# A transformer kernel's SwiGLU input stages: a seed copied ahead of a SiLU, and the first stage's norm, low parts and gates reordered

## What is computed

```python
def swiglu(x, w_in, w_out):
    a, b = jnp.split(x @ w_in, 2, axis=-1)
    return (jax.nn.silu(a) * b) @ w_out

for i in range(DEPTH_2):
    h = h + FFN_RES * swiglu(rmsnorm(h, g_ff1[i]), w_ff1_in[i], w_ff1_out[i])
    h = h + hybrid_mixer(rmsnorm(h, g_mix[i]), ...)
    h = h + FFN_RES * swiglu(rmsnorm(h, g_ff2[i]), w_ff2_in[i], w_ff2_out[i])
    ...
```

## Time and profile before

| | us |
|---|---|
| median of 3 runs | 2997.67 |
| lowest and highest | 2995.54, 3002.64 |
| the profiled execution, device time | 2998.98 |
| its span in the trace | 2997.0 |
| TensorE busy | 2900.9 (97%) |
| VectorE busy | 2123.1 (71%) |
| ScalarE busy | 1396.3 (47%) |
| mean granted TensorE clock | 0.988 |

### The profile page before, as it was taken

The page is one execution under the profiler, slowest core; times in us unless marked ns, Lnnn a source line. Parts: engine busy times, 40 slices in busy tenths (PEclk is TensorE's granted clock), DMA queues, the critical chain, the costliest instruction groups (busy, mean ns, idle before and its releaser), DMA issues. The chain is left out here.

```text
span 2997.0 us, 50791 instructions
## 1 busy us (share of the span) xinstructions
PE 2900.9 (97%) x18548; PEld 2500.2 (83%) x18548; DVE 2123.1 (71%) x3185; ACT 1396.3 (47%) x2309; POOL 455.9 (15%) x356
## 2 busy tenths in 40 slices
PE   7999999889999999999999999999999999999998
PEld 3888888777789988777799988799888777899886
DVE  5677776355689745887699845899547886899545
ACT  3645555454356522334466522566323335566422
POOL 0113112184600011000300012100110000200012
PEclk9999999999999999999999999999999999999998
DMA  6212022123223222322232323233222222323322
GB/s 258 62 44 63 24 55 59 36 81 117 99 88 112 97 98 81 98 92 77 98 107 98 115 88 112 71 112 99 100 89 92 92 78 87 110 98 112 104 95 74
DMA packets 97244, 275.10 MB, mean 92 GB/s; under 512 B 35712, under 2 KB 36864, under 8 KB 95760
## 3 DMA queue, kind: packets, MB, share of 16 engines
q1 hardware_dynamic: 94016, 267.89, 27.3%
q10 hardware_dynamic: 2768, 4.25, 0.5%
q0 software_dynamic: 320, 1.05, 0.1%
HBM read 267.88 MB, written 5.28 MB: 91 GB/s over the span
## 5 line engine op out<-in xcount | busy, mean ns | idle before, releaser
L142 DVE TENSOR_TENSOR weights_lo<-weights_raw,weights_hi 128x1024 fp32r<-128x1024 f32 (+2 forms) x258 | 397.6, 1541 | 326.2 <-ACT weights_hi L137 322.7
L137 ACT ACTIVATE weights_hi<-weights_raw 128x1024 fp32r<-128x1024 f32 (+2 forms) x250 | 285.3, 1141 | 431.8 <-PE bank L151 424.7
L149 PE MATMUL bank<-x_hi,weights_hi 128*128 128x512 f32 x832 | 336.9, 405 | 4.6 <-DVE x_lo L1943 2.7
L151 PE MATMUL bank<-x_hi,weights_lo 128*128 128x512 f32 x832 | 326.4, 392 | 0.0
L150 PE MATMUL bank<-x_lo,weights_hi 128*128 128x512 f32 x832 | 325.2, 391 | 0.0
L2053 PE MATMUL bank<-sum_hi,block_hi 128*128 128x256 f32 x960 | 271.2, 282 | 13.7 <-ACT bank L2194 9.6
L149 PE MATMUL bank<-hidden_hi,weights_hi 128*128 128x512 f32 x704 | 273.9, 389 | 0.0
L150 PE MATMUL bank<-hidden_lo,weights_hi 128*128 128x512 f32 x704 | 273.9, 389 | 0.0
L151 PE MATMUL bank<-hidden_hi,weights_lo 128*128 128x512 f32 x704 | 273.9, 389 | 0.0
L2054 PE MATMUL bank<-sum_lo,block_hi 128*128 128x256 f32 x960 | 270.8, 282 | 0.0
L2055 PE MATMUL bank<-sum_hi,block_lo 128*128 128x256 f32 x960 | 269.9, 281 | 0.0
(11 more groups left out here) (437 smaller groups left out, 7322.6 us busy)
## 6 DMA issues: line engine op xcount, KB each, us to landing
raw_pair<-w_ff1in SPq DMA_DIRECT2D x42, 1024.0 KB, 4.9
raw_pair<-w_ff2in SPq DMA_DIRECT2D x42, 1024.0 KB, 4.9
weights_raw<-w_mix SPq DMA_DIRECT2D x72, 512.0 KB, 3.5
weights_raw<-w_ff1out SPq DMA_DIRECT2D x32, 704.0 KB, 4.0
weights_raw<-w_ff2out SPq DMA_DIRECT2D x32, 704.0 KB, 4.1
weights_raw<-w_tail SPq DMA_DIRECT2D x42, 512.0 KB, 3.5
mod_weights<-w_mod SPq DMA_DIRECT2D x6, 2048.0 KB, 16.7
weights_raw<-w_dn SPq DMA_DIRECT2D x24, 512.0 KB, 3.7
```

Source lines behind the costliest of these rows:

```text
L137: nc.scalar.activation(K.wh[:, slot, 0:cols], K.raw[:, slot, 0:cols], ACT.Copy).then_inc(S.wh_ready, 1)
L142: nc.vector.tensor_tensor(K.wl[:, slot, 0:cols], K.raw[:, slot, 0:cols], K.wh[:, slot, 0:cols].bitcast(F32), ALU.subtract).then_inc(S.raw_ ...
L149: nc.tensor.matmul(out, K.wh[:, slot, a:b], xh, start=start, stop=False)
L151: return nc.tensor.matmul(out, K.wl[:, slot, a:b], xh, start=False, stop=stop)
```

## The change

Six things are done.

1. ScalarE, all four stages: in pair 3 `seed_a` comes ahead of `fourth_hi` and `silu(2)` (`second=True`). For that pairs 3 and 4 are written out ahead of the loop, which now starts at 1.
2. The banks of the plain pair 1 are exchanged: projection 2 goes to bank 5 and projection 3 to bank 3, and `scale_plain` and `gate_plain` read them there. So `evac`, for which the seed of pair 3 waits, covers the last reader of banks 4 and 5, to which it copies.
3. VectorE, stages 2 to 4: `second` of pair 3 comes ahead of its `first_lo`.
4. VectorE, stage 1: a new order, with the reciprocal first and the gates of pairs 0 and 1 among the work of pair 3.
5. ScalarE, stage 1: a new order to match; the load of SiLU's table comes after the first two splits.
6. The activation that brings the table in writes to a tile of its own (`unread`) and no more to `fifth_product`.

```diff
@@ -319,6 +319,7 @@
     K.ident = put("identity", [128, 128])
     K.ones = put("ones", [128, 128])
     K.eps = put("eps", [128, 1])
+    K.unread = put("unread", [128, 1])
     K.banks = ctx.enter_context(nc.psum_tensor("bank", [128, 4096], F32))
     K.pb = [K.banks[:, 512 * i:512 * i + 512] for i in range(8)]
     return at
@@ -2038,14 +2039,14 @@
         if q > 0:
             pe_sum_squares(pe, q)
         project(1, 4, False)
-        project(2, 3, False)
+        project(2, 5, False)
         if q == 0:
             pe_sum_squares(pe, q)
             K.final_pe(pe)
 
         for bank in (1, 2):
             nc.tensor.matmul(pb[bank][:, :], K.identr[:, :], xgh[:, 0, :], start=True, stop=True)
-        project(3, 5, False)
+        project(3, 3, False)
 
         def product(out, hi, lo, x, start=False):
             for k in range(4):
@@ -2149,7 +2150,7 @@
             nc.scalar.activation(K.t1[:, :], K.t1[:, :], ACT.Silu).then_inc(S.silu_ready, 1)
 
         def silu_table():
-            nc.scalar.activation(K.s5[:, 0:1], K.eps[:, 0:1], ACT.Silu)
+            nc.scalar.activation(K.unread[:, 0:1], K.eps[:, 0:1], ACT.Silu)
 
         def hidden_hi(j):
             act.wait_ge(S.g_ready, FT * f + j + 1 + CREDIT)
@@ -2203,10 +2204,19 @@
             act.wait_ge(S.product_done, left("product_done") + 5 * number(j) + product)
             nc.scalar.activation(half_out(p, name), half_out(p, "a_right"), ACT.Copy).then_inc(S.seeded, 1)
 
-        def half_pair(j, p, end=False):
-            fourth_hi(j)
-            silu(j - 1)
-            seed_a(j, p)
+        def half_pair(j, p, end=False, second=False):
+            if second:
+                seed_a(j, p)
+                if q == 0:
+                    silu(1, True)
+                    plain_block_hi(j, p)
+                    hidden_hi(1)
+                fourth_hi(j)
+                silu(j - 1)
+            else:
+                fourth_hi(j)
+                silu(j - 1)
+                seed_a(j, p)
             keep_fifth(j)
             seed_b(j, p, "b_left", 3)
             hidden_hi(j - 1)
@@ -2224,6 +2234,20 @@
 
             first_hi(j, p, True)
             plain_block_hi(j, p)
+            if q == 0:
+                silu_table()
+                second_hi(j, True)
+                seed_a(j, p)
+                silu(0, True)
+                keep_fifth(j, True)
+                sum_hi(4)
+                seed_b(j, p, "b_left", 3)
+                fourth_hi(j)
+                seed_b(j, p, "b_right", 5)
+                first_hi(j + 1, 1 - p)
+                hidden_hi(0)
+                second_hi(j + 1)
+                return
             silu(0, True)
             second_hi(j, True)
             seed_a(j, p)
@@ -2249,9 +2273,12 @@
             act_std(act, q)
             K.final_act(act)
         sum_hi(3)
-        silu_table()
+        if q > 0:
+            silu_table()
         first_half_pair(PLAIN_PAIRS, 0)
-        with act.Fori(0, HALF_PAIRS // 2 - 1) as i:
+        half_pair(PLAIN_PAIRS + 1, 1, second=True)
+        half_pair(PLAIN_PAIRS + 2, 0)
+        with act.Fori(1, HALF_PAIRS // 2 - 1) as i:
             for p in (1, 0):
                 half_pair(2 * i + PLAIN_PAIRS + 2 - p, p)
         half_pair(FT - 1, 1, end=True)
@@ -2311,13 +2338,13 @@
         def scale_plain(j):
             dve.wait_ge(S.slab_done, s0 + 2 * j + 1 + CREDIT)
             dve.wait_ge(S.g_ready, FT * f + j + CREDIT)
-            nc.vector.tensor_tensor(K.t1[:, :], pb[3 * j][:, :], rstd[:, :], ALU.mult).then_inc(S.evac, 2)
+            nc.vector.tensor_tensor(K.t1[:, :], pb[5 * j][:, :], rstd[:, :], ALU.mult).then_inc(S.evac, 2)
 
         def gate_plain(j):
             dve.wait_ge(S.slab_done, s0 + 2 * j + 2 + CREDIT)
             dve.wait_ge(S.silu_ready, FT * f + j + 1 + CREDIT)
             dve.wait_ge(S.hid_ready, FT * f + j + CREDIT)
-            nc.vector.tensor_tensor(K.t2[:, :], pb[4 + j][:, :], K.t1[:, :], ALU.mult).then_inc(S.g_ready, 1)
+            nc.vector.tensor_tensor(K.t2[:, :], pb[4 - j][:, :], K.t1[:, :], ALU.mult).then_inc(S.g_ready, 1)
 
         def sum_b(j, p, end=False):
             dve.wait_ge(S.slab_done, s0 + 2 * j + (2 if end else 1) + CREDIT)
@@ -2398,13 +2425,34 @@
         def first_half_pair(j, p):
 
             differences(j, p)
+            if q == 0:
+                dve_rstd(dve, q, v0)
+                first_lo(j, p)
+                second(j, p)
+                fourth(j, p)
+                scale_plain(0)
+                second_lo(j)
+                plain_block_lo(j, p)
+                sum_lo(3)
+                sum_lo(4)
+                fourth_lo(j)
+                differences(j + 1, 1 - p)
+                gate_plain(0)
+                first_lo(j + 1, 1 - p)
+                second(j + 1, 1 - p)
+                scale_plain(1)
+                hidden_lo(0)
+                second_lo(j + 1)
+                gate_plain(1)
+                fourth(j + 1, 1 - p)
+                hidden_lo(1)
+                sum_b(j, p)
+                scale_a(j, p)
+                return
             second(j, p)
             fourth(j, p)
-            if q == 0:
-                first_lo(j, p)
             dve_rstd(dve, q, v0)
-            if q > 0:
-                first_lo(j, p)
+            first_lo(j, p)
             scale_plain(0)
             plain_block_lo(j, p)
             gate_plain(0)
@@ -2416,8 +2464,8 @@
             sum_lo(4)
             differences(j + 1, 1 - p)
             fourth_lo(j)
+            second(j + 1, 1 - p)
             first_lo(j + 1, 1 - p)
-            second(j + 1, 1 - p)
             fourth(j + 1, 1 - p)
             hidden_lo(1)
             second_lo(j + 1)
```

## The result

The changed kernel takes **3025.73 us** (median of 4 runs, lowest and highest 3022.91 and 3026.95) against 2999.26 for the kernel before, run beside it: a ratio of 1.0087, 95% interval 1.007 to 1.0105. It is slower, where 2986 was forecast as 0.4% faster. The range, 2980.5 to 2993, missed it by 33 us.

The account below looks back on a forecast made before the run. TensorE, busy 97% of the span, was taken as the bound, losing time only to waits or lower clock. Gains of 5.2 + 3 x 1.75 + 1.5 = 12.0 us off 2997.67 gave 2985.7, forecast as 2986; range 2980.5 to 2993.

Parts of the forecast that it names:

- (d): Straight-line code: if each of eight unrolled ScalarE pairs paid 2.2 us on the path, slower, 3003 us; chance 0.04.
- Seed ahead, stages 2 to 4: Pair 3's product 3 no longer waits 2.39 us for its seed: 1.75 us per stage, 1.5 more in stage 3.
- Stage 1, 5.2 us with one half clock: Stage 1 reordered: old waits go, a new 2.9 us wait precedes pair 3's product 4; 5.2 us gained with clock loss.
- The clock: TensorE's clock was let fall behind stage 1's new 2.9 us wait, costing 1.6; bounds of this unknown 0 and 1.5.
- Unrolled pairs at nothing: ScalarE's pairs 3 and 4 written ahead of its loop: between 0 and 2.2 us per pair, taken as 0.
- Sum 12.0: Total gain: 5.2 for stage 1, 3 x 1.75 for stages 2 to 4, and 1.5 for stage 3's clock, 12.0 us.
- Range: 2980.5 to 2993 us: ends from costs, 2984.6 and 2990.2, widened in part by the spread of the three runs before.
- (a): Stage 1 gives its gain back through longer VectorE waits for ScalarE: 7.5 us gained in all, 2990; chance 0.13.
- (b): Stages 2 to 4: VectorE's swap brings nothing, a stage gives 1.05 us; sum 9.9, 2988; chance 0.10.
- (c): Seed wait goes, but the clock falls elsewhere in stages 2 to 4, 1.5 us each: 2987.5 to 2989; chance 0.10.

Follow-up runs that it names:

- seed alone: Packed kernel with stage 1 otherwise in its old order, keeping the seed ahead of SiLU in all four stages: 2991.2 us, ratio 0.9975 against the kernel before.
- packed kernel: The changed kernel with the tile `unread` put inside the 32 bytes that `eps` takes up, so no other tile moves: 2986.16 us, ratio 0.9953 against the kernel before.
- the last run above: Repeat of the fastest kernel with pair 4's seed also copied ahead of its SiLU: 2970.95 us, ratio 0.9905 against the kernel before.
- stage 1 alone: Packed kernel with stages 2 to 4 in the old order, pairs 3 and 4 still unrolled: 3000.22 us, ratio 1.0 against the kernel before.
- With 64 bytes: The changed kernel with `unread` 64 bytes long in place of 32: 2991.03 us, ratio 0.9968 against the kernel before.
- the last four traces: Two runs each of the fastest kernel (2958.01, 2959.96 us) and of it with pair 4's seed ahead of SiLU (2976.76, 2970.95 us).
- the fastest kernel: Packed kernel with `block_*` 32 bytes higher, `plain_block_*` 32 lower, first block's tiles from keys_queries on 96 higher: 2958.01 us, ratio 0.9861 against the kernel before.

## Why the prediction was wrong

**The failed step is a term that isn't in the sum.** The prediction costed the seed, stage 1 and the unrolled pairs, and gave item 6 of the change, the tile, no cost and no bounds. It stands in one line of the diff and looked like bookkeeping. It was worth +33 us alone and +39 in the changed kernel, against the -12 of everything else. None of the rivals had it either: (d), the one on the slower side, put the loss into straight-line code.

Point by point, against the kernel in which the tile does not move the others:

- *Seed ahead, stages 2 to 4, 1.75 us each and 1.5 more in stage 3*: right. 202.0 became 200.2 in stages 2 and 4 and 203.5 became 200.2 in stage 3, so 1.8, 3.3 and 1.8. The wait of 2.39 is gone; product 4 of pair 3 waits 0.15 where 0.3 was worked out, and product 3 of pair 4 waits 0.2 where 0.5 was.
- *Stage 1, 5.2 us with one half clock*: right in size, 5.1, with a wait of 2.92 where 2.9 was worked out, at 843.67 where 844.25 was. The reasons were half right. The seed alone gave 4.8 of it, in an execution whose clock held in stage 1; the new order there, which took most of the working, exchanges waits of 1.4 and 2.8 for one of 2.9.
- *The clock*: of one mind with the rows, but too sure. It fell behind the 2.92 of the packed kernel and held behind the same 2.92 in the last run above. It did not fall behind 2.78 in the kernel with the seed alone, and fell in stage 2 with stage 1 alone, whose waits for the seed are 2.3 at the longest, where it had not before. So half clock followed waits of 2.3 to 2.9 in some executions and not in others.
- *Unrolled pairs at nothing*: right, no idle time for no reason appeared, and stages 2 to 4 are as short as worked out.
- *Sum 12.0*: 817.2 less 805.2 is 12.0, which is the firm part. That the medians meet as well, 2986.16 for 2985.7, is in part luck, since executions differ by more ahead of stage 1.
- *Range*: its low end, 2980.5, lies 4.1 below the 2984.6 from the costs, twice the 2.1 by which the runs before lie below their median, and not a part of it. With the right ends the result would have missed it as well.
- Rivals (a) to (d) did not occur. (b) and (c) differ from the forecast by 3 us at most and would hardly have been told from it by times; the stage lengths tell them.

The sign was wrong since the step of a matmul, 0.227 and 0.118, was taken as a constant of the kernel and read from the trace before. The reader could have asked what in the change could alter it: a list of what the layout does to addresses would have shown that the moving tiles of these products move and the weights and blocks do not. No row of the trace before priced that. The nearest was in plain sight, though: in the first block of the kernel before, the matmuls on `mixed_*`, whose tiles lie partly at place 32, step by 0.233 and not 0.227.

## What to carry to other kernels

A declaration is an edit. Where memory is laid out by hand, list the addresses of matmul operands before and after, and if the distance between a stationary and a moving tile changes, give that a term with bounds of both signs: here 32 bytes cost 3% on the matmuls of 512 columns on weights, and 32 bytes in the right place gave 4% on those of 256. When TensorE is busy 97% of the time, count matmuls in a stretch without waits and compare that first; the share of busy time and the list of waits do not show it, and the busy time in us shows a total without a cause. And compare stage by stage: the lengths of the four stages settled to 0.3 us what the medians left open by 5.

## What the runs showed of the hardware

- The step between back-to-back matmuls at full clock depends on where the operands lie. 512 columns took 0.226 to 0.238 us, 256 columns 0.113 to 0.120, with the same instructions. The Trainium skill ("SBUF — State Buffer", section "Operand start alignment") asks only for starts at a multiple of the element size, and says that this is about legality and not speed. All tiles here meet it, and the step differed all the same.
- For the pair of tiles, the distance modulo 128 bytes matters, not the place: 0 is the best and 32 and 96 the worst tried for 512 columns, 64 the best and 0 the worst for 256 on `block_*`. That it is distance is shown by moving both (2985.02 against 3025.73 us). Why, and by what exact law, is open: only steps of 32 bytes were tried, and the step on `plain_block_*` also goes by where the other blocks lie.
- With the same places a stage of products can run at 0.1135 or at 0.1175 us a matmul from beginning to end, by the execution. It was seen at a distance of 64, in 6 of 16 stages of the last four traces, and, for the plain blocks alone, in stage 4 of the kernel with all tiles 32 higher. With 64 bytes, at a distance of 32, `block_*` went from 117.0 in stage 2 to 117.6 and 117.9 in stages 3 and 4 of one execution. What decides it was not tried.
- In the fastest kernel VectorE is busy for 132.17 of 140 us in the products (columns: stretch, its length, busy time of TensorE, its loads, VectorE, ScalarE and GpSimd, granted clock, DMA share, GB/s), so by these rows little more can be had there from TensorE alone:

```profile
1540.00:1680.00 140.00, 140.00 (x1238) 140.00 (x1237) 132.17 (x178) 94.38 (x148) 0.00 (x0) 1.00 0.31 109
```
